# Output norms of heads 0 to 4: one pass of ones over a stacked high and low part

## The reference

```
o = o.transpose(1, 0, 3, 2, 4).reshape(B, S, H, V)
o = rmsnorm(o, out_gain)          # per head: o * rsqrt(mean(o*o, -1) + eps) * gain
o = o * jax.nn.silu(g).reshape(B, S, H, V)
```

## Time and profile before

| | us |
|---|---|
| median of 3 runs | 2095.19 |
| profiled execution | 2095.03 |
| its span, first to last instruction | 2093.2 |
| TensorE busy | 2083.4 |
| GpSimd busy | 1140.4 |
| VectorE busy | 1034.3 |
| ScalarE busy | 738.7 |

### The profile page before, as it was taken

How to read it: one execution, slowest core, us unless ns; L and a number is a source line. 1 busy time by engine, 2 the same in 40 slices (tenths; PEclk the granted TensorE clock), 3 DMA queues, 4 the chain that set the end, 5 groups by cost and what they waited for, 6 DMA issues and landing times.

```text
span 2093.2 us, 28354 instructions
## 1 busy us (share of the span) xinstructions
PE 2083.4 (100%) x11231; PEld 1738.1 (83%) x11231; DVE 1034.3 (49%) x1227; ACT 738.7 (35%) x869; POOL 1140.4 (54%) x821
## 2 busy tenths in 40 slices
PE   9999999999999999999999999999999999999998
PEld 8888888888888889888888888888888888888887
DVE  6487654555114356634555333744477544553225
ACT  6336532212224455543122233515433332122244
POOL 6677555555455433365555555544566455555553
PEclk9999999999999999999999999999999999999999
DMA  5222132222332222242222222322222222223321
GB/s 200 82 66 78 49 113 100 100 86 95 104 117 104 87 79 83 81 141 101 86 94 100 101 101 100 102 99 101 94 89 97 101 101 100 90 90 111 113 103 67
DMA packets 33228, 204.43 MB, mean 98 GB/s; under 512 B 3704, under 2 KB 6520, under 8 KB 9472
## 3 DMA queue, kind: packets, MB, share of 16 engines
q1 hardware_dynamic: 32496, 202.73, 28.1%
q10 hardware_dynamic: 656, 0.62, 0.1%
HBM read 200.19 MB, written 2.10 MB: 97 GB/s over the span
## 4 chain that ended last, share of the span: by engine, by line
PE 99%; DVE 0%; ACT 0%; issue 0%; DVEq 0%; POOL 0%; ACTq 0%; POOLq 0%
PE bank L2156 99%; DVE x L2014 0%; PE bank L2562 0%; PE bank L2453 0%; DVE h L2122 0%; ACT w_hi L853 0%; PE bank L2564 0%; ACT un L853 0%; PE bank L2588 0%; PE bank L2295 0%; ACT rr L853 0%; DVE ao_lo L1946 0%; ACT o_raw L853 0%; ACT ao_hi L853 0%; ACT rstd L853 0%
## 5 line engine op out<-in xcount | busy, mean ns | idle before, releaser
L712 POOL TENSOR_TENSOR w_lo<-raw,w_hi 128x512 fp32r<-128x512 f32 x676 | 975.9, 1474 | 856.7 <-ACT w_hi L853 856.7
L2156 PE MATMUL bank<-u_hi,w_hi 128*128 128x512 f32 (+1 forms) x1952 | 755.3, 387 | 0.1
L2156 PE MATMUL bank<-u_lo,w_hi 128*128 128x512 f32 (+1 forms) x1952 | 752.3, 386 | 0.0
L853 ACT ACTIVATE w_hi<-raw 128x2048 fp32r<-128x2048 f32 x185 | 354.4, 1915 | 913.0 <-PE bank L2156 909.0
L2156 PE MATMUL bank<-u_hi,w_lo 128*128 128x512 f32 (+1 forms) x1952 | 487.4, 386 | 0.0
L2156 PEld LDWEIGHTS bank<-u_hi,w_hi 128*128 128x128 f32 x1952 | 366.8, 188 | 73.9 <-ACTq L1278 0.5
L2156 PEld LDWEIGHTS bank<-u_lo,w_hi 128*128 128x128 f32 x1952 | 366.8, 188 | 73.0
L2156 PEld LDWEIGHTS bank<-u_hi,w_lo 128*128 128x128 f32 x1952 | 365.6, 188 | 73.9
L2156 PE MATMUL bank<-act_hi,w_hi 128*128 128x512 f32 x528 | 205.4, 389 | 0.0
L2156 PE MATMUL bank<-act_lo,w_hi 128*128 128x512 f32 x528 | 205.4, 389 | 0.0
L1427 DVE TENSOR_TENSOR h<-h,bank 128x512 f32<-128x512 f32 x48 | 30.8, 684 | 300.7 <-PE bank L2156 300.7
(11 more groups left out here) (319 smaller groups left out, 2117.2 us busy)
## 6 DMA issues: line engine op xcount, KB each, us to landing
raw<-wall SPq DMA_DIRECT2D x185, 1024.0 KB, 4.9
h<-x_t SPq DMA_DIRECT2D x3, 512.0 KB, 7.3
first_raw<-wall SPq DMA_DIRECT2D x6, 256.0 KB, 7.5
out_t<-h SPq DMA_DIRECT2D x6, 256.0 KB, 2.2
av_moved<-av SPq DMA_DIRECT2D x14, 64.0 KB, 2.1
h<-x_t SPq DMA_DIRECT2D x2, 256.0 KB, 3.6
first_raw<-wall SPq DMA_DIRECT2D x4, 128.0 KB, 3.5
lmask_f<-lmask_in SPq DMA_DIRECT2D x1, 512.0 KB
```

Of the source, the lines that this page charges most:

```text
L712: ins = nc.gpsimd.tensor_tensor(w_lo[:, s, c], raw[:, s, c], w_hi[:, s, c].bitcast(F32), ALU.subtract)
L853: return nc.scalar.activation(out, in_, func, **k)
L2156: return nc.tensor.matmul(out, lhsT, rhs, start=start, stop=stop, skip_group_check=True)
```

## The change

For heads 0 to 4 the 128 squares of a token are first added in pairs, partition q and partition q + 64. ScalarE squares the two halves of the PSUM bank apart, the upper one into `un[0:64, 1]` (the place of `sum_lo[1]`), and GpSimd adds them (`head_folded`). ScalarE copies the 64 sums to the lower half of `sum_hi[1]` as the high part (`folded_upper`, at step 3 instead of step 2), and GpSimd writes the low part to its upper half (`head_lower`). One pass of ones then adds both. The calls in GpSimd's queue are moved: `head_folded` stands where `head_lower` stood, or next to it, and `head_lower` comes later, behind a wait for GpSimd's own preceding work. Heads 5 to 7 keep the old way.

```diff
             def head_lower(hd):
                 pool.wait_ge(osq_upper, hd + 1)
+                if hd < LATE_HEADS:
+                    nc.gpsimd.tensor_tensor(sum_hi[1][HP:P, :], sq[0:HP, hd % 2, :], sum_hi[1][0:HP, :].bitcast(F32),
+                                            ALU.subtract).then_inc(osq_split, 1)
+                    pool.wait_ge(osq_split, hd + 1)
+                    return
...
+            def head_folded(hd):
+
+                if hd < LATE_HEADS:
+                    pool.wait_ge(osq_ready, hd + 1)
+                    total = sq[0:HP, hd % 2, :]
+                    nc.gpsimd.tensor_tensor(total, total, un[0:HP, 1, :], ALU.add).then_inc(osq_folded, 1)
...
                     fold_keys(p, 3)
                     if p:
+                        head_folded(2 * p - 2)
+                    lo_piece(8 + 3 * p, 0, 2)
+                    lo_piece(8 + 3 * p, 2, 4)
+                    if p:
+                        pool.wait_ge(lo_ready, 9 + 3 * p)
                         head_lower(2 * p - 2)
-                    lo_piece(8 + 3 * p, 0, 4)
                     fold_keys(p, 4)
                     fold_keys(p, 5)
                     decays(p + 1)
                     lo_piece(9 + 3 * p, 0, 2)
                     if p:
+                        head_folded(2 * p - 1)
+                    fold_keys(p, 6)
+                    if p:
+                        pool.wait_ge(kend_ready, (STEPS - 1) * p + 6)
                         head_lower(2 * p - 1)
-                    fold_keys(p, 6)
                     fold_keys(p, 7)
                 elif p < PAIRS - 1:
...
                     if p:
-                        head_lower(2 * p - 2)
+                        head_folded(2 * p - 2)
                     lo_piece(8 + 3 * p, 0, 2)
                     fold_keys(p, 4)
                     lo_piece(8 + 3 * p, 2, 4)
+                    if p:
+                        pool.wait_ge(lo_ready, 9 + 3 * p)
+                        head_lower(2 * p - 2)
                     fold_keys(p, 5)
                     decays(p + 1)
                     fold_keys(p, 6)
+                    if p:
+                        head_folded(2 * p - 1)
                     lo_piece(9 + 3 * p, 0, 2)
+                    fold_keys(p, 7)
                     if p:
+                        pool.wait_ge(kend_ready, (STEPS - 1) * (p + 1))
                         head_lower(2 * p - 1)
-                    fold_keys(p, 7)
                 else:
                     for l in range(1, STEPS):
                         fold_keys(p, l)
                         if l == 3:
+                            head_folded(2 * p - 2)
+                        elif l == 4:
+                            pool.wait_ge(kend_ready, (STEPS - 1) * p + 4)
                             head_lower(2 * p - 2)
...
                 if hd > 1:
                     act.wait_ge(oms_done, hd - 1)
+                if hd < LATE_HEADS:
+                    if hd:
+                        act.wait_ge(osq_folded, hd)
+                    af(sq[0:HP, hd % 2, :], tail_bank(hd)[0:HP, :], ACT.Square)
+                    af(un[0:HP, 1, :], tail_bank(hd)[HP:P, :], ACT.Square).then_inc(osq_ready, 1)
+                    return
...
+            def folded_upper(hd):
+                act.wait_ge(osq_folded, hd + 1)
                 if hd:
                     act.wait_ge(oms_done, hd)
-                af(sum_hi[1][:], sq[:, hd % 2, :], ACT.Copy).then_inc(osq_upper, 1)
+                af(sum_hi[1][0:HP, :], sq[0:HP, hd % 2, :], ACT.Copy).then_inc(osq_upper, 1)
...
                 elif step == 2:
                     head_squares(hd)
+                elif step == 3 and hd < LATE_HEADS:
+                    folded_upper(hd)
...
                 pe.wait_ge(osq_split, hd + 1)
-                mm(root_bank(hd)[:], ones_r[:], sum_hi[1][:], True, False)
-                mm(root_bank(hd)[:], ones_r[:], sum_lo[1][:], False, True).then_inc(oms_done, 1)
+                ins = mm(root_bank(hd)[:], ones_r[:], sum_hi[1][:], True, hd < LATE_HEADS)
+                if hd >= LATE_HEADS:
+                    ins = mm(root_bank(hd)[:], ones_r[:], sum_lo[1][:], False, True)
+                ins.then_inc(oms_done, 1)
```

More of the change, by code:

```diff
@@ L334, in build @@
         out_lo = sem("out_lo")
+        osq_folded = sem("osq_folded")
         osq_upper = sem("osq_upper")
@@ L1034, in head_squares @@
                     act.wait_ge(oms_done, hd - 1)
+                if hd < LATE_HEADS:
[4 more added lines that the diff above has]
+                    return
                 af(sq[:, hd % 2, :], tail_bank(hd)[:], ACT.Square).then_inc(osq_ready, 1)
                 act.wait_ge(osq_ready, hd + 1)
+                act.wait_ge(oms_done, hd)
+                af(sum_hi[1][:], sq[:, hd % 2, :], ACT.Copy).then_inc(osq_upper, 1)
+            def folded_upper(hd):
+                act.wait_ge(osq_folded, hd + 1)
                 if hd:
                     act.wait_ge(oms_done, hd)
-                af(sum_hi[1][:], sq[:, hd % 2, :], ACT.Copy).then_inc(osq_upper, 1)
+                af(sum_hi[1][0:HP, :], sq[0:HP, hd % 2, :], ACT.Copy).then_inc(osq_upper, 1)
             def root_log(hd):
```

## The result

| | before | changed |
|---|---|---|
| median, us (15 runs each, side by side on one chip) | 2095.57 | 2100.34 |
| lowest to highest, us | 2094.59 to 2097.40 | 2096.39 to 2103.12 |
| ratio of times, 95% interval | | 1.0021 (1.0014 to 1.0028) |
| profiled execution, us | 2095.03 | 2096.39 |
| its span, us | 2093.2 | 2094.6 |

The forecast was 2096.4, with 2093.9 to 2098.5 around it. The changed kernel is 4.8 us slower than before by the medians, and the prediction was wrong. The profiled execution took 2096.39 us, 0.2 above the 2096.20 that the sum gives for it, and it is also the lowest of the kernel's 15 runs. So there are two questions: whether the terms of the sum hold in the profile, and what the other runs have that this one lacks.

The account below looks back on a forecast made before the run. The prediction took TensorE's queue to bound the kernel from end to end. Five passes less (1.20 us) and two stalls more (1.16 and 1.21) gave 2096.20 on the profiled run, 2096.4 against the median, range 2093.9 to 2098.5.

Parts of the forecast that it names:

- the sum: Whole kernel: profiled 2095.03 us, minus 1.20 for passes, plus stalls of 1.16 and 1.21, gives 2096.20; against the median, 2096.4.
- The passes: TensorE in the mixer: five passes of ones against `sum_lo` removed, 0.24 us each, 1.20 us saved.
- Two stalls of the forecast's kind: TensorE waits for GpSimd's late low part: 1.16 us at head 0, 1.21 us at head 2.
- no gap at heads 1, 3 and 4: Mixer: the low parts of these heads would be ready before TensorE asks, so no stall there.
- The self-wait: GpSimd, ahead of the low part: waiting for its own preceding work adds 0.17 us.
- the margin: Head 3: low part ready at 199.38, TensorE asks at 200.37, so 1.0 us in hand.
- the nil margin: `fold_keys(3, 1)` ends at 204.93, level 2 of the last pair needs it at 204.91; no stall counted, up to 0.4 us.
- the price of half the partitions: GpSimd's 64-partition fold and subtract: 1.29 us each taken, as at 128 partitions; 0.65 and 2.03 for the range.
- VectorE pays: Rival, chance 0.04: added GpSimd work slows VectorE and through it TensorE by 6.45 us, giving 2102.8.
- The cover named for level 4 of head 0's pair: VectorE's `next_keys` ends 0.77 us ahead of TensorE's level 4, covering some 0.3 us of longer wait.
- the first one: Whole kernel: TensorE's queue is the time end to end; only fewer TensorE cycles or new waits change it.
- the rivals: No stall, 2094.0 (0.14); change ineffective, 2097.6 (0.02); GpSimd's chain tips over, 2098 to 2100 (0.10); VectorE slowed, 2102.8 (0.04).

Follow-up runs that it names:

- late_low: The kernel before, full width and two passes, with the low parts of heads 0 and 2 made as late as in the change; 2098.44 us, ratio 1.0013.
- early: The changed kernel with the low parts of heads 0 and 2 made two pieces earlier; 2094.64 us, ratio 0.9995.
- one_stall: The changed kernel with only head 0's low part made two pieces earlier, head 2's staying late; 2099.39 us, ratio 1.0008.
- head0_gap: The changed kernel with only head 2's low part made two pieces earlier, head 0's staying late; 2096.47 us, ratio 1.0000.
- again3: The changed kernel unchanged, run once more on a third chip; 2102.23 us, ratio 1.0030.
- again: The changed kernel unchanged, run again for a second profile; 2098.52 us, ratio 1.0010.
- early_pad8: The changed kernel with low parts of heads 0 and 2 two pieces earlier, plus 8 always-met waits ahead of each of five passes; 2095.89 us, ratio 0.9996.
- early2: The changed kernel with low parts of heads 0 and 2 two pieces earlier, run once more on a second chip; 2096.80 us, ratio 1.0003.
- later_sum: The changed kernel with TensorE's passes for heads 0 and 2 asked for two slices later; 2096.01 us, ratio 1.0001.
- early_pad: The changed kernel with low parts of heads 0 and 2 two pieces earlier, plus 2 always-met waits ahead of each of five passes; 2096.61 us, ratio 1.0001.
- pad_two: The changed kernel with 2 always-met waits ahead of each of the five passes; 2100.93 us, ratio 1.0015.
- again2: The changed kernel unchanged, run once more on a second chip; 2100.53 us, ratio 1.0018.

## Why the prediction was wrong, step by step

**What held.** The passes: five matmuls fewer. Two stalls of the forecast's kind, at heads 0 and 2, and no gap at heads 1, 3 and 4. The span of the first profile grew by 1.4 us, and the sum says 1.17. late_low, early, one_stall and head0_gap bear out the cause: each gap goes and comes with the place of one low part.

**What was mis-sized there.** The stalls. The idle times of 1.10 and 1.33 us look like the forecast's 1.16 and 1.21, but they are another quantity: they count from the recorded end of the last product, while the forecast counts from the start that the pass would have had. Before, the pass starts 0.69 us behind the start of the six products ahead of it, at both heads:

```profile
135.54 0.94 PE L2156 MATMUL bank<-val,ssq 128*128 128x128 f32 x6
...
181.87 0.94 PE L2156 MATMUL bank<-val,ssq 128*128 128x128 f32 x6
```

with the passes at 136.23 and 182.56. In the changed kernel these products start at 135.34 and here:

```profile
182.54 0.94 PE L2198 MATMUL bank<-val,ssq 128*128 128x128 f32 x6
```

So the passes would have started at 136.03 and 183.23. They start at 137.38 and 184.80, 1.35 and 1.57 late, which is 0.55 us more than forecast. late_low has the same surplus: 2.2 of idle time and 2.7 of span. The sum with them would be 2.92 - 1.20 = 1.72. The span grew by only 1.4, since TensorE came to head 0 already 0.20 us earlier than before (135.34 against 135.54), which has nothing to do with the change. That the profile came so near the sum is in part luck.

The fold on 64 partitions takes 1.28 to 1.29 us, as taken. The low part doesn't: by the rows of its tile it is 1.28 at best and 1.52 in the median.

```profile
L780 POOL TENSOR_TENSOR sum_hi<-sq,sum_hi x5: 1280/1523/1626, 135.8 to 218.3; 64x512 fp32r<-64x512 f32 x5
```

This is 0.2 to 0.3 us more than the 1.29 taken for heads 0 and 2. The self-wait that should have added 0.17 shows only 0.08 (130.46 + 5.26 = 135.72 to 135.80), so part of it cancels. From the low part's end to the pass another 0.06 and 0.14 us go by, for which the sum has no term. At head 3 the margin was 0.24 (199.20 + 1.28 = 200.48 against 200.72) where I had 1.0: the key fold ahead of it took 2.03, not 1.54, and the two pieces ahead of that 3.0, not 2.64. `fold_keys(3, 1)` ended at 205.14, 0.1 ahead of the level at 205.25, the nil margin that was counted as no stall. On the price of half the partitions the Trainium skill ("GPSIMD Engine Reference", section "Architecture") agrees with these rows: 1.28 to 1.29 for 64 partitions, 1.29 for 128.

**VectorE pays.** It did not. DVE's busy time rose by 5.8 us in all, near the 6.45 of that rival, and none of it reached TensorE, whose waits in its first profile have no VectorE line beyond the one it had the earlier trace rows. The cover named for level 4 of head 0's pair held.

**The step that failed** is the first one and the line of the sum that rests on it: "the time is TensorE's queue from end to end", and the profiled time plus 0.16 as the median. That step let the kernel grow only by waits of TensorE on other engines. The rows of one execution don't hold two costs that other executions pay, and none of the rivals had them.

The first is the stop of 2.0 us inside pair 3's products, when the next 16 KB of instructions is fetched only as TensorE runs out of them. It stands in three of four profiles of the changed kernel, all but the first, and in neither of before's two. The second is the 1.7 us that the fall of the clock costs. It isn't the change's own: before's runs beside the experiments have a mean clock of 0.998 or less in 52 of 125. The changed kernel's have it in 31 of 44. The stop is a second place for a fall (again3), but again's runs have it in 9 of 11 and mostly lie too low for a stop, so why it is more frequent isn't shown. The first profile has neither cost.

The runs' own clocks bear out both sizes. In before's 125 runs the median is 2095.36 where the mean clock is 0.999, and 2097.20 where it is lower. In the changed kernel's 15, ten runs have 0.998 and took 2100.25 to 2103.12, median 2100.8. Five have 0.999 and took 2096.39 to 2099.42, median 2099.0. So the clock is worth 1.8 us in either kernel, and four runs at 0.999 lie 2.5 to 3.0 us above the one that is known to lack the stop.

For the medians this gives 1.4 by the rows, 2.0 by the stop and 1.7 by the clock: the changed kernel's median run has a mean clock of 0.998, and before's median of 2095.57 lies with the runs at 0.999 (its own clock isn't on record). That makes 5.1, and 4.8 were measured. Which single runs had the stop is read from the profiled ones alone. For the others it is inferred from how the runs lie: a group at 2100 and above that is there in the kernels with the stop in their profile, and missing with 8 or 16 waits added.

**What stays open.** Why the block is fetched late. No other engine's lateness explains it: up to the stop, the other engines' instructions run in again as in the first profile, shifted with TensorE. That the stop sits at a fixed place in the program is shown, and that it is in none of the four profiles with 8 or 16 waits a pass. For early, whose two profiles without them lack it as well, early_pad8 says little. That the gap at head 2 makes it more likely is only a count: in the profiles of kernels with one pass, unpadded or with 2 waits, it appears in 5 of 6 with that gap and in 1 of 5 without it (early, early2, head0_gap, later_sum, early_pad). The same program gave both, so the place doesn't decide it alone either. What makes the clock fall in some runs behind the attention stage's 1.9 us wait and not in others stays open too.

## What to carry to other kernels

Where one engine's queue is the time, two gaps of about a microsecond can be forecast from the trace to 0.2 to 0.4 us, and moving one instruction ahead of two others took them away. Measure such a stall from start to start against the kernel before, not by the idle time in the bracket. Ask first for the place in the queue and only then for the work saved. The rows of one execution need not be those of a kernel's median (the first profile of the changed kernel is the lowest of 15 runs, again's the highest of 11): take a second profile of the same program, and hold the profiled time against all of its runs, before a sum of one microsecond is trusted. Put a range on what recurs in only some executions, here 2 us of instruction supply and 1.7 us of clock, each about as large as the whole effect that was being predicted.

## What the runs showed of the hardware

- TensorE can run out of instructions in a dense stretch of small matmuls. In 0.69 us it went through 56 products 128x16, then stood for 2.0 us, with a 16 KB block of instructions arriving around the start of the stop and nothing else on the DMA queues in that slice (again). In all six profiles with such a stop it lasts 2.0 to 2.3 us. The Trainium skill ("Runtime: NRT & Kernel Launch", section "Instruction fetch mechanics") describes the fetch as sequential prefetch that stays hidden behind the engine's issue. Over most of the kernel the traces agree; at this one place, in six of the 18 profiles, they don't.
- The granted clock fell from 2.4 to 1.2 GHz for 3.4 us after TensorE had stood for 1.9 us in the attention stage, in some executions and not in others of the same program (in 12 of the 18 profiles). It also fell at the end of the stop in again3, one_stall and pad_two, but not in again, again2 or early_pad.
- A GpSimd sum on 64 partitions took 1.28 to 1.29 us, as long as the subtract on 128 (1.28 to 1.30). The 64-partition subtract into the upper half of a tile took 1.28 to 1.63.
